# A top-k by bitwise search and matmuls in place of a top-k by maxima, and the next expert's transposes issued ahead of the down products

## The chip, the cores and the metric

One core of one Trainium2 chip. The metric is the device time of one launch in microseconds (us). All arithmetic is in float32. The engines are TensorE (PE; its weight loads are listed as PEld), VectorE (DVE), ScalarE (ACT), GpSimd (POOL) and SyncE (SP), which issues most of the DMAs. Each engine runs its own instruction stream; they meet at semaphores (`then_inc`, `wait_ge`).

## The reference

One layer of a diffusion backbone over 2048 tokens of width 1024: modulated RMSNorm, three token mixers (gated DeltaNet, Hyena, short convolution), a gated residual, and then the part that the change is about, an expert-choice mixture of experts (16 experts, 256 tokens each), followed by a final RMSNorm.

```python
def expert_choice_moe(h, router_w, w_gate, w_up, w_down):
    cap = CAPACITY_FACTOR * n // N_EXPERTS                      # 2 * 2048 // 16 = 256
    aff = jax.nn.softmax((h @ router_w).astype(jnp.float32), axis=-1)
    top_val, top_idx = lax.top_k(jnp.swapaxes(aff, 1, 2), cap)  # each expert takes its 256 best tokens
    xe = h[bidx, top_idx]
    hid = jax.nn.silu(jnp.einsum('becd,edf->becf', xe, w_gate)) * jnp.einsum('becd,edf->becf', xe, w_up)
    ye = jnp.einsum('becf,efd->becd', hid, w_down) * top_val[..., None].astype(h.dtype)
    return jnp.zeros_like(h).at[bidx, top_idx].add(ye.astype(h.dtype))
```

The order of an expert's 256 tokens doesn't matter to the output, since each row is added back to its own token.

## The kernel before

The kernel is a sequence of blocks; each ends with a barrier of all engines. Three of them matter here.

The **mixer's output stage** (L1720 to L1907) goes over 16 tiles of 128 tokens. TensorE makes `merged @ w_out` in two halves (`out_half`), VectorE and GpSimd form the new residual `x1` and the normalised row `h2`, TensorE transposes `h2` (`turn`, L1782) and makes the 16 router logits (`route`, L1792), VectorE and ScalarE the softmax in `ex` (L1841 to L1847). `turn_aff` transposes the 128x16 result (L1799), and VectorE copies it into `affT`, 16 experts by 2048 tokens (L1858). SyncE stores `x1` and `h2` in DRAM (`x1_d`, `h2_d`).

The **expert block** (from L1910) starts with the top-k. VectorE goes 32 times round `max` (the 8 largest of each of the 16 rows, L1951), `max_index` (where they are, L1954) and `match_replace` (they become -1, L1957). ScalarE copies each 8 values and 8 indices (L1986, L1987) to `vals` and `idxf`. TensorE transposes the lists with four small products (L2005, L2006), and VectorE copies them to `idxP` and `valP`, two columns of 128 tokens per expert (L1959, L1960).

Then sixteen experts, two per turn of a loop. GpSimd gathers an expert's 256 rows of `h2_d` with two indirect DMAs (L2050), one expert ahead. TensorE transposes them (16 transposes into banks 0 to 3, L2017), ScalarE copies them to the single buffer `xeT` (L1995), TensorE makes gate and up for six slices `f` of the hidden width, 32 instructions each, in banks 4 and 5 (L2025); ScalarE makes the sigmoid (L1999), VectorE two products (L1967, L1969) to `hid`. TensorE makes four down products of 6 x 2 instructions in banks 6 and 7 (L2036), VectorE scales them with the router value `valP` and the gate into `ye` (L1975), and GpSimd adds the rows to `x1_d` with two indirect DMAs (L2061). SyncE loads the weights: gate and up (3 MB each) are double buffered in `wgu`, down (3 MB) is single in `wd`; `wgu_free` and `wd_free` are raised by TensorE when it is done with a buffer (L1933, L1935). A float32 product is two weight loads and two passes on TensorE, a transpose one.

The **last block** reads `x1_d` back, normalises and stores.

The order on TensorE within an expert is the order of the code:

```python
pe.wait_ge(xe_in[b], i * 32 + 32)      # rows gathered
...                                    # 16 transposes
pe.wait_ge(xe_cp, at * 4 + 8)          # ScalarE's four copies
pe.wait_ge(wgu_in[b], i * 32 + 32)
...                                    # gate and up
pe.wait_ge(wd_in, at * 16 + 16)
pe.wait_ge(hid_ok, at * FT + FT + 2)   # VectorE's last hid
...                                    # down
```

## Time and profile before

| | us |
|---|---|
| median of 3 runs (lowest to highest) | 5180.27 (5178.26 to 5183.38) |
| the profiled execution, its own time | 5179.65 |
| its span in the profile | 5178.1 |
| TensorE busy | 4342.4 (84%) |
| VectorE busy | 1385.6 (27%) |
| ScalarE busy | 815.8 (16%) |
| GpSimd busy | 733.5 (14%) |
| DMA | 468 MB, 90 GB/s on average |

In the rows, a group reads: line, engine, operation, written tile <- read tiles, shapes, count | busy us, mean ns of one | idle time of the engine before them and what ended it. A line of the timeline is start, length, engine, line, operation, with the idle time before it in brackets. "x48" in a timeline is that many instructions run together. The granted clock is a share of full speed: 1.00 is 2.4 GHz, 0.50 is 1.2 GHz.

### The profile page before, as it was taken

To read this page: it belongs to the slowest core of one execution; us is meant where nothing else is said; L and a number is where in the kernel's file an instruction comes from. 1 tells how busy PE (TensorE), PEld (TensorE's weight loads), DVE (VectorE), ACT (ScalarE), POOL (GpSimd) and SP (SyncE) were. 2 spreads that over 40 slices of the span, in tenths; PEclk is the share of its full clock that TensorE was granted. 3 is DMA by queue.
4 is the path that set the end of the run, shared out by engine and by line. 5 is a ranking of instruction groups with operands and counts; after the bars stand their busy time and mean duration, and the time that the engine had idled before them with its cause. 6 is when DMAs were issued, how large, how long until landed. Compare 5 with 4: busy or idle time off the path is not lost. (4 is left out here: it accounts for less than half of the span.)

```text
span 5178.1 us, 49192 instructions
## 1 busy us (share of the span) xinstructions
PE 4342.4 (84%) x17543; PEld 2720.7 (53%) x17543; DVE 1385.6 (27%) x2250; ACT 815.8 (16%) x1538; POOL 733.5 (14%) x663
## 2 busy tenths in 40 slices
PE   7588888799999999877299999989900999999993
PEld 5344443599999844333144444435500777666662
DVE  1422222354555412232300000002289111111112
ACT  0244334122222111001100000001100000000002
POOL 0022233122222200001200000002200000000000
PEclk9799999899999999989599999999955999999997
DMA  6321111111111100254410000023330355554444
GB/s 239 135 61 49 48 53 46 63 53 57 61 53 61 53 25 14 67 157 124 148 33 27 24 26 26 24 68 134 113 130 1 105 178 178 178 178 169 161 151 142
DMA packets 253186, 468.13 MB, mean 90 GB/s; under 512 B 18964, under 2 KB 124092, under 8 KB 252992
## 3 DMA queue, kind: packets, MB, share of 16 engines
q1 hardware_dynamic: 218399, 366.54, 20.9%
q0 software_dynamic: 20560, 70.83, 5.0%
q10 hardware_dynamic: 14160, 29.89, 1.7%
q8 instruction: 40, 0.66, 0.1%
q14 instruction: 27, 0.21, 0.0%
HBM read 356.57 MB, written 110.62 MB: 90 GB/s over the span
## 5 line engine op out<-in xcount | busy, mean ns | idle before, releaser
L1666 PE MATMUL bank<-hT,gw 128*128 128x512 f32 x1536 | 678.6, 595 | 14.6 <-DMA bw<-in_w_branch_c 11.2
L2025 PE MATMUL bank<-xeT,wgu 128*128 128x256 f32 x3072 | 669.1, 380 | 14.6 <-ACT xeT L1995 14.6
L2025 PEld LDWEIGHTS bank<-xeT,wgu 128*128 128x128 f32 x3072 | 583.7, 190 | 97.5 <-issue 18.5
L500 PE MATMUL bank<-hT,wq 128*128 128x512 f32 (+1 forms) x1216 | 512.7, 577 | 9.6 <-DMA wq<-in_w_in 7.3
L1666 PEld LDWEIGHTS bank<-hT,gw 128*128 128x128 f32 x1536 | 292.2, 191 | 386.2 <-issue 386.2
L500 PEld LDWEIGHTS bank<-hT,wq 128*128 128x128 f32 x1216 | 237.1, 198 | 255.2 <-issue 249.2
L2036 PE MATMUL bank<-wd,hid_e 128*128 128x512 f32 x768 | 333.9, 594 | 22.1 <-DVE hid_e L1969 22.1
L1168 PE MATMUL bank<-hT,wh 128*128 128x512 f32 x768 | 336.4, 597 | 12.5 <-DMA wh<-in_w_in 9.4
L1697 DVE TENSOR_TENSOR pr<-sg_m,bank 128x512 f32<-128x512 f32 x96 | 66.0, 687 | 833.2 <-ACT sg_m L1682 833.2
L2036 PEld LDWEIGHTS bank<-wd,hid_e 128*128 128x128 f32 x768 | 144.6, 190 | 204.6 <-issue 176.0
L1168 PEld LDWEIGHTS bank<-hT,wh 128*128 128x128 f32 x768 | 145.6, 191 | 196.9 <-issue 196.9
L1773 PE MATMUL bank<-wo,mt 128*128 128x512 f32 x512 | 227.4, 598 | 16.4 <-DMA wo<-in_w_out 16.4
L884 PE MATMUL bank<-Eb,TT 128*128 128x128 f32 x1728 | 218.2, 279 | 20.3 <-DVE Eb L1086 20.3
L884 PE MATMUL bank<-Tb,N 128*128 128x128 f32 x1728 | 228.0, 277 | 0.3 <-ACT Tb L974 0.3
L884 PEld LDWEIGHTS bank<-Eb,TT 128*128 128x128 f32 x1728 | 206.8, 191 | 23.9 <-DVE Eb L1086 23.4
L1967 DVE TENSOR_TENSOR gm<-sgm,bank 128x256 f32<-128x256 f32 x96 | 40.4, 421 | 658.3 <-ACT sgm L1999 658.3
L884 PEld LDWEIGHTS bank<-Tb,N 128*128 128x128 f32 x1728 | 209.5, 192 | 3.6 <-ACT Tb L974 3.6
L2005 PE MATMUL bank<-eye,idxf 16*128 16x16 f32 x2 | 0.5, 273 | 239.6 <-ACT idxf L1987 239.6
L978 ACT ACTIVATE TT<-bank 128x512 f32<-128x512 f32 x216 | 129.0, 597 | 392.0 <-PE bank L890 389.5
L1682 ACT ACTIVATE sg_m<-bank 128x512 f32<-128x512 f32 x96 | 57.3, 597 | 780.0 <-PE bank L1669 779.9
L600 POOL TENSOR_SCALAR sg<-tmp 128x512 f32<-128x512 f32 (+1 forms) x76 | 104.6, 1376 | 508.3 <-DVE tmp L663 429.4
L2061 POOL DMA_INDIRECT x_d<-ye,idc x32 | 51.2, 1599 | 843.4 <-DVE ye L1975 843.4
(279 smaller groups left out, 4846.5 us busy)
## 6 DMA issues: line engine op xcount, KB each, us to landing
wgu<-in_exp_w_gate SPq DMA_DIRECT2D x16, 3072.0 KB, 23.1
wgu<-in_exp_w_up SPq DMA_DIRECT2D x16, 3072.0 KB, 30.4
wd<-in_exp_w_down SPq DMA_DIRECT2D x16, 3072.0 KB, 13.4
ada<-in_ada_w SPq DMA_DIRECT2D x12, 2048.0 KB, 8.9
gw<-in_w_in SPq DMA_DIRECT2D x27, 512.0 KB, 5.6
fa_d<-az ACTq DMA_DIRECT2D x48, 264.0 KB
sp_in<-fa_d SPq DMA_DIRECT2D x66, 192.0 KB, 4.1
kT<-kT_d SPq DMA_DIRECT2D x36, 256.0 KB, 2.8
```

Source lines behind the costliest of these rows:

```text
L500: last = pe.matmul(PS[u % 4][:, 0:width(n)], wq[:, kind, k, :], hT[:, k, toff(n):toff(n) + width(n)], start=(k == 0), stop=(k == KD - 1))
L600: pool.tensor_scalar_max(sg[:, u % 4, 0:w], tmp[:, u % 4, 0:w], CLAMP).then_inc(clamp_ok, 1)
L884: last = pe.matmul(b4(bank)[:, h, :], lhsT[:, h, :], rhs[:, h, :] if len(rhs.shape) == 3 else rhs, start=True, stop=True)
L978: act.activation(flat(TT, e), PS[2 * (e % 2) + 1][:, :], ACT.Copy).then_inc(TT_ok, 1)
L1168: last = pe.matmul(PS[u % 4][:, :], wh[:, kind, k, :], hT[:, k, toff(n + 1):toff(n + 1) + TW], start=(k == 0), stop=(k == KD - 1))
L1666: pe.matmul(g[:, :], gw[:, b, j, k, :], hT[:, k, toff(n + 1):toff(n + 1) + TW], start=(k == 0), stop=(k == KD - 1))
L1682: act.activation(sg[:, u % 2, :], PS[u % 4 * 2][:, :], ACT.Sigmoid).then_inc(sg_ok, 1)
L1697: dve.tensor_tensor(pr[:, u % 4, :], sg[:, u % 2, :], PS[u % 4 * 2 + 1][:, :], ALU.mult).then_inc(pr_ok, 1)
L1773: last = pe.matmul(PS[2 * (t % 2) + c][:, :], mt[:, t // 2 % 2, k, t % 2 * P:(t % 2 + 1) * P], wo[:, k, c * 512:(c + 1) * 512], start=(k = ...
L2025: last = pe.matmul(PS[4 + f % 2][:, g * CAP:(g + 1) * CAP], wgu[:, b, g, k, f * P:(f + 1) * P], xeT[:, k, :], start=(k == 0), stop=(k == K ...
L2036: last = pe.matmul(PS[6 + c][:, :], hid[:, f, j * P:(j + 1) * P], wd[:, f, c * 512:(c + 1) * 512], start=(f == 0), stop=(f == FT - 1))
L2061: pool.indirect_dma_start(x1_d, bass.IndirectOffsetOnAxis(idc[:, b, j:j + 1], 0), ye[:, j, :], None, compute_op=ALU.add).then_inc(ye_st, 16)
```

## The change

It has three parts.

1. In the mixer's output stage the softmax is kept by tile in `aff` (128 x 16 tiles x 16 experts); `turn_aff`, `ex` and `affT` are gone. A table `rt` (128 x 1104) is loaded. Rows of `h2_d` are 1040 long: the expert block stores a token's 16 router values behind its 1024 elements, so that a gather brings them along and `valP` is gone.
2. The top-k: `threshold` finds each expert's 256th largest value bit by bit. The values are laid out 128 wide, so that partition p holds expert p % 16. In each of 30 rounds VectorE compares 256 values per partition with a candidate and counts, TensorE adds the counts over the partitions of one expert with a block matrix, and VectorE keeps the bit or not. `slots` gives each chosen token its place in the list by products with triangular and counting matrices. `one_hot` and `listed`, each for eight experts, turn places into lists of token numbers: place = 16 * high + low, and a product of two one-hot matrices puts the token number at (high, low).
3. The experts: `turn`, the transposes of the next expert, is issued after gate/up and ahead of the down products. `xeT` has two buffers. The last two experts stand outside the loop.

```diff
# mixer's output stage
-                        pe.transpose(PS[7][0:NE, 0:P], ex[:, t % 2, :], eye[:, :]).then_inc(aff_tr, 1)
-                            dve.tensor_copy(affT[:, (t - 2) * P:(t - 1) * P], PS[7][0:NE, 0:P]).then_inc(affT_ok, 1)
+                    sp.dma_start(rt[:, :], A["t_rt"]).then_inc(rt_in, 16)
-                        sp.dma_start(h2_d[t * P:(t + 1) * P, :], h2[:, t % HB, :]).then_inc(h2_st[t % HB], 16)
+                        sp.dma_start(h2_d[t * P:(t + 1) * P, 0:D], h2[:, t % HB, :]).then_inc(h2_st[t % HB], 16)
# expert block, SyncE, ahead of the weight loads
+                    sp.dma_start(h2_d[:, D:D + NE].rearrange("(t p) e -> p t e", p=P), aff[:, :, :]).then_inc(aff_st, 16)
# VectorE: threshold
+                        for i in range(BITS):                     # BITS = 30
+                            bit = 1 << (BITS - 1 - i)
+                            c, nxt = cand[:, i % 3, :], cand[:, (i + 1) % 3, :]
+                            if i >= 1:
+                                dve.wait_ge(cand_ok, i)
+                            dve.tensor_scalar(hits[:, 0:2, :], affS[:, :, :], c.bitcast(F32), 0.0, ALU.is_ge, ALU.add, accum_out=votes[:, :]).then_inc(voted, 1)
+                            dve.tensor_scalar(nxt, c, bit | bit >> 1, None, ALU.bitwise_xor).then_inc(pair_ok, 1)
+                            dve.tensor_scalar(up[:, :], c, bit >> 1, None, ALU.bitwise_or).then_inc(pair_ok, 1)
+                            dve.wait_ge(vote_mm, i + 1)
+                            dve.tensor_scalar(full[:, :], PS[1][:, 0:1], CAP - 0.5, None, ALU.is_ge).then_inc(full_ok, 1)
+                            dve.wait_ge(full_ok, i + 1)
+                            dve.wait_ge(pair_ok, 2 * i + 2)
+                            dve.copy_predicated(nxt, full[:, :], up[:, :]).then_inc(cand_ok, 1)
# VectorE: slots (thrB, four counts, cntB, two masks, then eleven chained instructions of 128x256 or 128x512)
+                        for g, op in enumerate((ALU.is_gt, ALU.is_equal)):
+                            for h in range(2):
+                                dve.tensor_scalar(hits[:, 2 * g + h, :], affS[:, h, :], thr, 0.0, op, ALU.add, accum_out=cnt[:, 2 * g + h:2 * g + h + 1]).then_inc(cnt_ok, 1)
...
+                        link(dve.tensor_tensor(least[:, :, :], ties, wanted, ALU.min))
...
+                        link(dve.tensor_copy(digf[:, :], digu[:, :]))
# VectorE: one_hot(g), listed(g)
+                        for a in range(16):
+                            dve.scalar_tensor_tensor(hotA[:, :, :, a], high, float(a), index, ALU.is_equal, ALU.mult).then_inc(hot_ok, 1)
+                        for b in range(16):
+                            dve.tensor_scalar(hotB[:, :, :, b], low, float(b), None, ALU.is_equal).then_inc(hot_ok, 1)
...
+                        dve.tensor_tensor(own[:, :, :], PS[5][:, 0:P].rearrange("p (e b) -> p e b", b=16), own_e, ALU.mult).then_inc(z_ch, 1)
...
+                        dve.tensor_copy(idxP[:, :, g * 8:(g + 1) * 8], PS[6][:, 0:16].rearrange("p (j e) -> p j e", j=2)).then_inc(slots_ok, 1)
...
+                    threshold(); slots(); one_hot(0); listed(0); one_hot(1); listed(1)
+                    dve.sem_inc(hid_ok, 2)
# VectorE, experts
-                                dve.scalar_tensor_tensor(ye[:, j, c * 512:(c + 1) * 512], PS[6 + c][:, :], valP[:, j, ds(at, 1)], g2,
+                                dve.scalar_tensor_tensor(ye[:, j, c * 512:(c + 1) * 512], PS[6 + c][:, :], xe[:, b, j, ds(at + D, 1)], g2,
# TensorE
+                        for i in range(BITS):
+                            pe.wait_ge(voted, i + 1)
+                            pe.matmul(PS[1][:, 0:1], rt[:, T_BLK:T_BLK + P], votes[:, :], start=True, stop=True).then_inc(vote_mm, 1)
...
+                        for g in range(2):                        # slots
+                            for h in range(2):
+                                pe.matmul(PS[3 + g][:, 0:17 * NE], cntB[:, 2 * g + h, :], rt[:, (T_E0, T_E1)[h]:(T_E0, T_E1)[h] + 17 * NE], start=(h == 0), stop=False)
+                        for g in range(2):
+                            pe.wait_ge(mask_ok, g + 1)
+                            pe.matmul(PS[3 + g][:, 0:TILES * NE], rt[:, T_SU:T_SU + P], mask[:, g].rearrange("p t e -> p (t e)"), start=False, stop=True).then_inc(pos_mm, 1)
+                    def lists(g):
+                        pe.wait_ge(hot_ok, 32 * g + 32)
+                        for t in range(TILES):
+                            last = pe.matmul(PS[5][:, 0:P], hotA[:, t].rearrange("p e a -> p (e a)"), hotB[:, t].rearrange("p e b -> p (e b)"),
+                                             start=(t == 0), stop=(t == TILES - 1))
+                        last.then_inc(list_mm, 1)
+                        pe.wait_ge(spread_ok, g + 1)
+                        pe.matmul(PS[6][:, 0:16], spread[:, :, :].rearrange("p r b -> p (r b)"), rt[:, T_PLACE:T_PLACE + 16], start=True, stop=True).then_inc(idx_mm, 1)
...
+                    def expert(i, b, more):
+                        at = i * 2 + b
+                        pe.wait_ge(xe_cp, at * 4 + 4)
+                        pe.wait_ge(wgu_in[b], i * 32 + 32)
...                                                               # gate and up as before
+                        if more:
+                            turn(i + b, 1 - b, at + 1)
+                        pe.wait_ge(gu_mm, at * FT + FT)
+                        pe.sem_inc(wgu_free, 1)
+                        pe.wait_ge(wd_in, at * 16 + 16)
+                        pe.wait_ge(hid_ok, at * FT + FT + 2)
...                                                               # down as before
+                    threshold(); slots(); lists(0); turn(0, 0, 0); lists(1)
+                    with pe.Fori(0, NE // 2 - 1) as i:
+                        for b in range(2):
+                            expert(i, b, True)
+                    expert(NE // 2 - 1, 0, True)
+                    expert(NE // 2 - 1, 1, False)
# GpSimd, ahead of the first gather
                     pool.wait_ge(slots_ok, 1)
+                    pool.wait_ge(aff_st, 16)
```

ScalarE follows the same order: the six sigmoids of an expert, then the four copies of the next expert's transposes.

## Rows read from the trace of the kernel before

**Rows 1.** The page: 40 slices, busy tenths and granted TensorE clock.
```profile
PE   7588888799999999877299999989900999999993
...
PEclk9799999899999999989599999999955999999997
```

**Rows 2.** Windows: stretch, us, busy by engine, clock, DMA share, GB/s.
```profile
3700.00:3750.00 50.00, 50.00 (x173) 26.45 (x172) 10.73 (x24) 9.28 (x24) 14.09 (x6) 1.00 0.23 84
3800.00:3810.00 10.00, 0.00 (x0) 0.00 (x0) 9.32 (x8) 0.31 (x2) 0.00 (x0) 0.50 0.98 382
3810.00:3850.00 40.00, 0.00 (x0) 0.00 (x0) 37.20 (x28) 1.84 (x12) 0.00 (x0) 0.50 0.00 0
```

**Rows 3.** Timeline (start, us, instruction) around the top-k stage's two ends.
```profile
3767.24 0.23 DVE L1847 TENSOR_SCALAR ex<-ex,sm 128x16 f32<-128x16 f32 x1
...
3767.53 0.38 PE L1799 MATMUL bank<-eye,ex 128*16 128x128 f32 x1 [1.32 <-DVE ex L1847]
3767.95 0.28 DVE L1858 COPY affT<-bank 16x128 f32<-16x128 f32 x1 [0.47 <-PE bank L1799]
3768.82 0.40 SPq L1933 DMA_DIRECT2D wgu<-in_exp_w_gate  x1
...
4009.41 0.17 DVE L1959 CAST idxP<-bank 128x32 uint32<-128x32 f32 x1
4009.51 0.17 DVE L1960 COPY valP<-bank 128x32 f32<-128x32 f32 x1
...
4017.79 3.67 PE L2017 MATMUL bank<-eye,xe 128*128 128x128 f32 x16 [9.64 <-DMA xe<-h_d,idc]
...
4022.23 1.22 PE L2025 MATMUL bank<-xeT,wgu 128*128 128x256 f32 x2 [0.77 <-ACT xeT L1995]
```

**Rows 4.** Groups of the top-k stage: count, busy us, mean ns, idle before.
```profile
L1951 DVE MAX8 m<-affT 16x8 f32<-16x2048 f32 x32 | 73.0, 2282 | 8.7 <-DVE affT L1957 7.5 <-DVEq L1939 1.3
...
L1957 DVE MATCH_REPLACE8 affT<-m,affT 16x2048 f32<-16x2048 f32 x32 | 72.5, 2264 | 0.0
...
L1954 DVE MATCH_VALUE_LOAD i<-m,affT 16x8 f32 x32 | 2.5, 79 | 4.7
```

**Rows 5.** Timeline of TensorE's products over three experts.
```profile
4067.23 20.87 PE L2036 MATMUL bank<-wd,hid_e 128*128 128x512 f32 x48 [1.39 <-DVE hid_e L1969]
4088.40 1.97 PE L2017 MATMUL bank<-eye,xe 128*128 128x128 f32 x16 [0.30 <-PE bank L2036]
4091.29 41.70 PE L2025 MATMUL bank<-xeT,wgu 128*128 128x256 f32 x192 [0.92 <-ACT xeT L1995]
4134.38 20.87 PE L2036 MATMUL bank<-wd,hid_e 128*128 128x512 f32 x48 [1.38 <-DVE hid_e L1969]
4156.07 1.96 PE L2017 MATMUL bank<-eye,xe 128*128 128x128 f32 x16 [0.83 <-PE bank L2036]
```

**Rows 6.** The page: DMA issues, KB each, median us to landing.
```profile
wd<-in_exp_w_down SPq DMA_DIRECT2D x16, 3072.0 KB, 13.4
```

**Rows 7.** Groups of VectorE by shape.
```profile
L1967 DVE TENSOR_TENSOR gm<-sgm,bank 128x256 f32<-128x256 f32 x96 | 40.4, 421 | 658.3 <-ACT sgm L1999 658.3
...
L418 DVE TENSOR_SCALAR xb<-xb,ss 128x1024 f32<-128x1024 f32 x18 | 12.4, 749 | 15.6 <-ACT ss L397 15.6
...
L277 DVE TENSOR_SCALAR turns<-arg 64x512 f32<-64x512 f32 x8 | 3.4, 419 | 0.3
...
L762 DVE TENSOR_TENSOR gx<-gl,dtb 128x160 f32<-128x160 f32 x1 | 0.3, 325 | 0.0
...
L759 DVE TENSOR_SCALAR beta<-gl 128x160 f32<-128x160 f32 x1 | 0.2, 244 | 0.0
```

**Rows 8.** Timeline at the mixer stage's tail, TensorE at half clock.
```profile
3762.61 3.49 PEld L1792 LDWEIGHTS bank<-rw,h2T 128*128 128x128 f32 x16 [1.58 <-ACT h2T L1878]
...
3766.81 0.19 ACT L1871 ACTIVATION_READ_ACCUMULATOR ex<-bank,mx 128x1 f32 x1
```

**Rows 9.** Timeline of GpSimd: the second gather of expert 2.
```profile
4102.98 0.95 POOL L2050 DMA_INDIRECT xe<-h_d,idc  x1 [0.30 <-issue]
```

More of the change, by code:

```diff
@@ L1719, in build @@
         fst = top.enter_context(ExitStack())
-        affT = sbt(fst, "affT", [NE, SEQ])
+        aff = sbt(fst, "aff", [P, TILES, NE])
+        rt = sbt(fst, "rt", [P, N_RT])
+        rt_in = sem("rt_in")
         fgb = sbt(fst, "fgb", [P, D])
@@ L1815, in _ @@
                             out_half(t, 1)
-                        if t >= 2:
-                            turn_aff(t - 2)
                         if 1 <= t <= TILES:
@@ L1924, in build @@
             dn_mm, ye_ok, ye_st, ye_free = sem("dn_mm"), sem("ye_ok"), sem("ye_st"), sem("ye_free")
+            hits = gm1[:, :, :].rearrange("p a (b t) -> p (a b) t", t=P)
+            cntB = sgm[:, :, :].rearrange("p a (b t) -> p (a b) t", t=P)
+            mask = hid[:, 0:2, :].rearrange("p g (t e) -> p g t e", e=NE)
+            least, slot, chosen = [hid[:, r, :].rearrange("p (t e) -> p t e", e=NE) for r in (2, 3, 4)]
+            own, spread = [hid[:, 5, h * P:(h + 1) * P].rearrange("p (e b) -> p e b", b=16) for h in range(2)]
+            hotA = ye[:, :, :].rearrange("p j (t e a) -> p (j t) e a", e=8, a=16)
+            hotB = xeT[:, 1, :, :].rearrange("p k (t e b) -> p (k t) e b", e=8, b=16)
             with nc.Block() as block:
@@ L1962, in _ @@
+                    threshold()
+                    slots()
+                    one_hot(0)
+                    listed(0)
+                    one_hot(1)
+                    listed(1)
+                    dve.sem_inc(hid_ok, 2)
                     with dve.Fori(0, NE // 2) as i:
@@ L2001, in _ @@
+                    with act.Fori(0, NE // 2 - 1) as i:
+                        for b in range(2):
+                            expert(i, b, True)
+                    expert(NE // 2 - 1, 0, True)
+                    expert(NE // 2 - 1, 1, False)
                 @block.tensor
                 def _(pe):
[L2003 to L2006 removed]
@@ new lines, in threshold @@
+                    def threshold():
+                        for h in range(2):
+                            last = pe.transpose(PS[0][:, h * P:(h + 1) * P], aff[:, h * 8:(h + 1) * 8, :].rearrange("p t e -> p (t e)"), eye[:, :])
+                        last.then_inc(affS_tr, 1)
+                        pe.wait_ge(rt_in, 16)
+                        for i in range(BITS):
+                            pe.wait_ge(voted, i + 1)
+                            pe.matmul(PS[1][:, 0:1], rt[:, T_BLK:T_BLK + P], votes[:, :], start=True, stop=True).then_inc(vote_mm, 1)
@@ new lines, in turn, with expert @@
+                    def turn(i, b, at):
+                        pe.wait_ge(xe_in[b], i * 32 + 32)
+                        for k2 in range(KD // 2):
+                            for k in (2 * k2, 2 * k2 + 1):
+                                for j in range(2):
+                                    last = pe.transpose(PS[k2][:, (k % 2 * 2 + j) * P:(k % 2 * 2 + j + 1) * P], xe[:, b, j, k * P:(k + 1) * P], eye[:, :])
+                            last.then_inc(xe_tr, 1)
+                    def expert(i, b, more):
+                        at = i * 2 + b
+                        pe.wait_ge(xe_cp, at * 4 + 4)
+                        pe.wait_ge(wgu_in[b], i * 32 + 32)
+                        for f in range(FT):
+                            pe.wait_ge(hid_ok, at * FT + f + 1)
+                            for g in range(2):
+                                for k in range(KD):
+                                    last = pe.matmul(PS[4 + f % 2][:, g * CAP:(g + 1) * CAP], wgu[:, b, g, k, f * P:(f + 1) * P], xeT[:, b, k, :],
+                                                     start=(k == 0), stop=(k == KD - 1))
+                            last.then_inc(gu_mm, 1)
+                        if more:
+                            turn(i + b, 1 - b, at + 1)
[3 more added lines that the diff above has]
+                        pe.wait_ge(hid_ok, at * FT + FT + 2)
+                        for m in range(4):
+                            j, c = m // 2, m % 2
+                            if m >= 2:
+                                pe.wait_ge(ye_ok, at * 4 + m - 1)
+                            for f in range(FT):
+                                last = pe.matmul(PS[6 + c][:, :], hid[:, f, j * P:(j + 1) * P], wd[:, f, c * 512:(c + 1) * 512],
+                                                 start=(f == 0), stop=(f == FT - 1))
+                            last.then_inc(dn_mm, 1)
+                        pe.wait_ge(dn_mm, at * 4 + 4)
+                        pe.sem_inc(wd_free, 1)
@@ L2042, in _ @@
+                    threshold()
+                    slots()
+                    lists(0)
+                    turn(0, 0, 0)
+                    lists(1)
+                    with pe.Fori(0, NE // 2 - 1) as i:
+                        for b in range(2):
+                            expert(i, b, True)
+                    expert(NE // 2 - 1, 0, True)
+                    expert(NE // 2 - 1, 1, False)
                 @block.gpsimd
```

182 lines of the change are left out of this document (91 added, 91 removed).

## The prediction

> **What bounds the kernel now.** I read the page's 40 slices first: TensorE is busy nearly everywhere, except around the 30th slice, where its row shows 0 and 0 and its granted clock is 0.5 [rows 1]. The windows say what that stretch is: VectorE busy 37.2 of 40 us, TensorE and DMA 0 [rows 2]. The timeline of its two ends gives its length. The mixer stage's last instruction ends at 3767.95 + 0.28 = 3768.23; the first gate/up product of expert 0 starts at 4022.23 [rows 3]. So 254.0 us pass in which TensorE does four tiny transposes and one expert's 16. The groups say what fills them: VectorE instructions of 2.26 to 2.28 us, 32 times each, in a chain (L1951 and L1957; L1954's find is as long) [rows 4]. Behind it come sixteen experts on TensorE. There the PE timeline repeats every 67.15 us (down product to down product), 0.5 more where the loop turns back: 1.96 transposes, 0.92 idle behind ScalarE's last copy, 41.70 gate and up, 1.39 idle behind VectorE's last hid, 20.87 down, and 0.3 or (loop back) 0.8 idle [rows 5]. Nothing else is late there: the first 15.7 MB of weights took from 3768.8 to about 3810 [rows 2, 3], and wd lands a median 13.4 us after issue, with 46 us before its product [rows 5, 6]. TensorE's own order is therefore the path in the experts, VectorE's in the top-k.
>
> **Part 1, removed: the top-k by maxima.** The whole 254.0 us goes, and the new chain is built up below from the same start (3768.23).
>
> Entry into the block until the first instruction: 0.6, as SyncE's (3768.82). Two transposes and one 256-wide copy from PSUM: at half clock two weight loads are 0.22 apart (16 in 3.49), the product ends some 0.11 behind the last, and a copy of that size is 0.42 by the 256-wide rows: 1.0 with hand-offs.
>
> The search is 30 rounds of a closed loop between VectorE and TensorE. One round: (a) the compare of 128x256 with a [128,1] pointer and an accumulator. No row has this form. L277 (512 wide) took 0.419 and L759 (160 wide) 0.244, 0.5 ns a column; the two-input L762 (160) and L1967 (256) 0.325 and 0.421, 1 ns a column. L418 (1024 wide, with a pointer) took 0.749, 0.24 over its columns at 0.5 ns. So 256 columns are 0.37 at the fast rate and 0.50 at the slow one [rows 7]. (b) the accumulator read: between 0.08, the tiny VectorE instruction of rows 4, and 0.19, ScalarE's own accumulator read [rows 8]. (c) TensorE: hand-off 0.05, a product as two load-and-product pairs 0.55, hand-off 0.04 [rows 3, 8]. The two tiny candidate updates (0.17 each) run beside it. (d) the test of the count and the predicated copy, 0.17 each as the tiny L1959 [rows 3], and 0.04 to 0.08 for each wait. Sum: 0.37 to 0.50, 0.08 to 0.19, 0.64, 0.42 to 0.50: 1.5 to 1.8, and I take 1.6, for a one-input compare should go at the fast rate. Thirty: 48. Bounds: 1.25 if the product is prompt (0.35) and the read is free, 2.1 if each of the three waits on VectorE costs the 0.23 that L1951 shows behind its two waits (7.5 us in 32) [rows 4]: 37 to 63 us.
>
> Slots: threshold spread 0.15; four counts of 128 columns at about 0.42 = 1.7; spread 0.46; then TensorE. A 512-column pass goes every 0.43 us at full clock (48 in 20.87), so 272 columns at half clock are 0.46, eight of them 3.65, and four passes of 256 columns 1.72, with hand-offs 5.5. Behind it eleven chained VectorE instructions, mostly 256 wide at 0.42 and 0.04 apart [rows 7]: 4.3. Together 12.1 (10 to 15).
>
> One-hots of experts 0 to 7: sixteen two-input instructions of 128 columns and sixteen one-input. By L762 (160 wide, 0.325) and L759 (0.244) they are 0.29 and 0.23 long. They have no wait between them, and such rows overlap: L1959 and L1960 are 0.17 long and start 0.10 apart [rows 3, 7]. So 0.22 and 0.16, 6.1 us; I take 7 for strided writes. Against this the Trainium skill, VectorE: DVE Perf Modes, The DRAIN you can't avoid, says that the next instruction doesn't start before the pipe is empty; by that the sum would be 8.3. The pair of rows disagrees with it, by 0.07 us per instruction, so I keep 7.
>
> Lists of experts 0 to 7: 16 products of 128 columns, two pairs each at 0.22: 7.1 at half clock. Their reduction: three VectorE instructions of about 0.33, a product 0.6, a copy 0.17: 1.8 with its waits. Now GpSimd may gather; from the copy's end to expert 0's transposes took 4017.79 - 4009.68 = 8.1, and the transposes 3.7 [rows 3]. Experts 8 to 15 have their one-hots made meanwhile (7 or 8.3, hidden in 11.8), but their products stand behind expert 0's transposes in TensorE's queue, and hid_ok is raised only after them: 7.1 + 1.8 more before the first gate/up product. ScalarE's copies of expert 0 lie beside that.
>
> Sum: 0.6 + 1.0 + 48 + 12.1 + 7 + 7.1 + 1.8 + 8.1 + 3.7 + 7.1 + 1.8 = 98.3. The gain is 254.0 - 98.3 = **155.7**. Ends: 82 (votes 37, lists of the second half at full clock, fewer gaps) and 120.
>
> Two covers to check. The weights: expert 0's gate/up and down and expert 1's gate/up needed 41 us; the aff store (2,048 pieces of 64 B) goes ahead of them on SyncE's queue. Even if it costs 10 us they are in by 3820, against a first use at 3866. With the cover gone, had the new chain only the same 41 us, the store's whole 10 us would show. The table load (565 KB) lies behind wo's in the stage before.
>
> **Part 2, the mixer stage.** turn_aff and the affT copy go. TensorE is busy 50 of 50 us there [rows 2] and a transpose takes it about 0.11 us (16 in 1.97) [rows 5]: 14 x 0.11 = 1.5; one more at its tail, 0.1; and at the very end 3768.23 falls back to 3767.47, 0.76 [rows 3]. Together **2.4**. The h2 store, its rows now 4,160 B apart, is the same 4 KB per row.
>
> **Part 3, transposes ahead of the down products.** At the 15 boundaries TensorE now runs gate/up, the next 16 transposes, down, gate/up. Gone: the 0.92 behind ScalarE, because the copies lie under 20.87 us of down products, and the 1.39 behind VectorE, because the transposes fill it. They take 16 x 0.11 = 1.75 in a busy stream rather than 1.97, and start without the pipe draining. So down starts 1.6 to 1.75 instead of 1.39 after gate/up, and 1.96 + 0.92 disappear behind it: 2.5 to 2.65 each. Taking **2.5**: 15 x 2.5 = **37.5** (32 to 41). The 0.3 and 0.8 idle at the end of down stay; they come from waiting for its own product and the loop. Are the gathered rows there in time? The second was asked for at 4102.98, 15 us after the previous down ended [rows 5, 9], and takes about 6; the transposes now come 42 us after it. POOL's queue (scatter, wait for it, gather) is as before. SyncE's queue is unchanged in order; wgu_free comes 1.7 us later but SyncE stands at wd_free then. wd now has 43 us rather than 46 for its load. Reading the value from the gathered row costs the 0.75 us instruction nothing (a pointer either way), and 64 B more per row is 1.6%. The unrolled last pair replaces one loop turn.
>
> **Sum.** 155.7 + 2.4 + 37.5 = 195.6. The profiled execution took 5179.65 us (span 5178.1), 0.6 below the median 5180.27; the median's forecast is 5180.3 - 195.6 = 4984.7, say **4985**.
>
> **Rivals.**
> - *The hand-offs are dearer* (2.3 us and more per round: several semaphore waits in a row, an accumulator read that blocks). For it: 0.23 us behind two waits on VectorE [rows 4]; against it TensorE's 0.06 behind L1847 and VectorE's 0.04 behind TensorE [rows 3]. The Trainium skill, VectorE: DVE Perf Modes, Two Vector instructions with no wait between them, counts an accumulator output as two instructions; ScalarE's rows show the pair, and my (b) holds it. Time: 30 x 0.7 to 1.5 more, 5006 to 5030. Chance 0.14.
> - *The reorder gives nothing* in the experts: the transposes hold back down by what they save, or gate/up's loads wait. Against it, 0.92 and 1.39 are real idle time of TensorE [rows 5]. Time 4985 + 37 = 5022. Chance 0.05.
> - *The search is cheaper*: TensorE at full clock in the rounds, prompt products, 1.2 us each, lists at full clock: 98 falls to 80, 4966 and below. For it, the rounds give TensorE something to do; against it, no row shows the clock in such a loop, and the top-k stands at 0.50 [rows 1, 2]. Chance 0.09.
> - *Slower than before*: the gather comes late in the experts. Now transposes in front of down wait for it, and down with them. Down ended, the rows are in after some 21 us, against 42: it must come 21 us later before it costs anything, and 13 us at each of 15 boundaries more to eat 195. So above 5190 only from 34 us late on. Nothing on POOL's queue is new there. Chance 0.01.
> - *The maxima aren't the path*, the weights are: excluded by [rows 2], DMA is 0 from 3810 on. It would leave the top-k as it is, 5140; chance below 0.01.
>
> **How the numbers follow.** My forecast's chance is 0.70; its own range is 4968 to 5003 (votes 1.35 to 1.9, slots and lists +-4, boundaries +-4). The cheap and the dear search take the range to 4962 and 5010, which leaves out about 2 in 10. All cases but the fourth, and something unforeseen, are faster by over 0.2% (10 us, about what a measurement tells from no change): faster 0.97, same 0.01, slower 0.02.
>
> **What would show it.** From the stage's last softmax instruction to the first gate/up product some 98 us; rounds 1.6 us apart, with TensorE's part 0.6; a list product group of 7 us before and one after expert 0's transposes; gate/up starting 0.3 or 0.8 us after down; no idle before down; down-to-down 64.7 and 65.1. Wrong: rounds over 2 us, one-hots over 0.35 us each (two to four times 7 us), the second lists' one-hots later than the transposes, or a wait for xe in front of down.

## The result, and the profile after

| | before | after |
|---|---|---|
| median, us | 5181.83 (4 runs, 5178.26 to 5186.61) | 4975.4 (4 runs, 4970.01 to 4981.11) |
| ratio (95% interval) | | 0.9601 (0.9585 to 0.9618) |
| the profiled execution, its span | 5179.65, 5178.1 | 4970.01, 4968.5 |
| VectorE busy | 1385.6 | 1209.0 |
| TensorE busy | 4342.4 | 4362.6 |

The kernel became 206.4 us faster. The forecast of 4985 (4962 to 5010) is 9.6 us too high, and its sum of 195.6 us of gain is 14 us short of the 209.6 by which the profiled span shrank. The page after, 40 slices, busy tenths of TensorE and its granted clock:

```profile
PE   7588898699999999977639999999995999999993
...
PEclk9799999899999999999959999999996999999996
```

The two slices at 0, with clock 0.5, around the 30th in [rows 1] are now one slice of 5 tenths busy at 0.6. From here the traces are put beside each other by stage:

| stretch, us | before | after | gain | forecast |
|---|---|---|---|---|
| start to the mixer's output stage (unchanged code) | 3490.3 | 3487.6 | 2.7 | 0 |
| output stage, to its last instruction | 277.9 | 275.3 | 2.6 | 2.4 |
| top-k, to the first gate/up product | 254.0 | 91.6 | 162.4 | 155.7 |
| sixteen experts, to the last down product's end | 1076.4 | 1034.4 | 42.0 | 37.5 |
| tail | 79.5 | 79.6 | -0.1 | 0 |

The first line is the difference of two executions, not of two kernels: the output stage starts between 3487.6 and 3504.1 in the profiles of this study. The top-k stage repeats within 0.6 us and the experts within 0.1 wherever their code is the same, so the experiments are read by them.

The top-k stage in the timeline of the kernel after (start, length, engine, line): its start, one round of the search, the slots, the lists.

```profile
3762.67 0.23 DVE L1851 TENSOR_SCALAR aff<-aff,sm 128x16 f32<-128x16 f32 x1
...
3766.06 0.48 DVE L1974 TENSOR_SCALAR_CACHE_REDUCE gm<-affS,cand 128x256 f32<-128x256 f32 x1
3766.46 0.08 DVE L1974 DVE_READ_ACCUMULATOR gm<-affS,cand 128x1 f32 x1
...
3766.60 0.59 PE L2093 MATMUL bank<-votes,rt 128*128 128x1 f32 x2 [1.03 <-DVE gm L1974]
3767.23 0.16 DVE L1978 TENSOR_SCALAR full<-bank 128x1 uint32<-128x1 f32 x1 [0.55 <-PE bank L2093]
3767.42 0.22 DVE L1981 COPY_PREDICATED_SCALAR cand<-full,up 128x1 uint32 x1
3767.67 0.48 DVE L1974 TENSOR_SCALAR_CACHE_REDUCE gm<-affS,cand 128x256 f32<-128x256 f32 x1
...
3823.59 3.60 DVE L2019 SCALAR_TENSOR_TENSOR ye<-digf,rt 128x128 f32<-128x128 f32 x16
3827.03 2.29 DVE L2021 TENSOR_SCALAR xeT<-digf 128x128 f32<-128x128 f32 x16
3829.37 6.38 PEld L2109 LDWEIGHTS bank<-xeT,ye 128*128 128x128 f32 x32 [10.49 <-DVE xeT L2021]
3829.37 6.57 PE L2109 MATMUL bank<-xeT,ye 128*128 128x128 f32 x32 [10.09 <-DVE xeT L2021]
...
3837.49 0.17 DVE L2035 CAST idxP<-bank 128x16 uint32<-128x16 f32 x1 [0.49 <-PE bank L2113]
...
3845.99 3.30 PE L2120 MATMUL bank<-eye,xe 128*128 128x128 f32 x16 [8.54 <-DMA xe<-h_d,idc]
...
3849.14 3.74 PE L2109 MATMUL bank<-xeT,ye 128*128 128x128 f32 x32
...
3854.41 0.17 DVE L2035 CAST idxP<-bank 128x16 uint32<-128x16 f32 x1 [0.49 <-PE bank L2113]
...
3854.50 0.70 PE L2131 MATMUL bank<-xeT,wgu 128*128 128x256 f32 x2
```

The stage begins where L1851 ends, 3762.90, and ends at 3854.50. The round starts at 3766.06 and the next at 3767.67: 1.61 us. In it the compare and its accumulator read take 0.48, and 0.06 later TensorE's product begins, whose two pairs take 0.59. The test follows 0.04 later (0.16), then the copy (0.22 from 3767.42), and 0.03 behind it the next compare.

The experts, TensorE's timeline of the kernel after:

```profile
3854.50 41.71 PE L2131 MATMUL bank<-xeT,wgu 128*128 128x256 f32 x192
3896.05 1.91 PE L2120 MATMUL bank<-eye,xe 128*128 128x128 f32 x16
3897.79 20.77 PE L2145 MATMUL bank<-wd,hid_e 128*128 128x512 f32 x48
3919.10 41.70 PE L2131 MATMUL bank<-xeT,wgu 128*128 128x256 f32 x192 [0.54 <-PE bank L2145]
3960.64 1.91 PE L2120 MATMUL bank<-eye,xe 128*128 128x128 f32 x16
3962.38 20.77 PE L2145 MATMUL bank<-wd,hid_e 128*128 128x512 f32 x48
3984.02 41.70 PE L2131 MATMUL bank<-xeT,wgu 128*128 128x256 f32 x192 [0.87 <-PE bank L2145]
```

Against [rows 5]: no idle time in front of the transposes, none between them and the down products, none behind ScalarE's copies. What is left is 0.54, or 0.87 where the loop turns back, and its releaser is TensorE's own product. Down starts are 64.59 and 64.92 apart, where they were 67.15 and 67.6. The waits from 3854 to 4870 (total, times, longest) say how rare anything else is:

```profile
PE bank L2131 <- PE bank L2145: 9.7, 15, 0.9
...
PE bank L2145 <- DVE hid_e L2052: 1.5, 1, 1.5
```

The one wait for VectorE is the last expert's, which has no transposes behind its gate/up.

### The profile page after: what moved, and what is told of

The parts are those of the page before. It is cut to its first block and busy times, and to the rows that moved or that the text cites. A ratio compares the mean times of both kernels' runs of the same rounds, so it can differ in the third digit from the quotient of the medians.

```text
span 4968.5 us, 49038 instructions
## 1 busy us (share of the span) xinstructions
PE 4362.6 (88%) x17666; PEld 2748.0 (55%) x17666; DVE 1209.0 (24%) x2348; ACT 794.2 (16%) x1465; POOL 736.0 (15%) x664
## 3 DMA queue, kind: packets, MB, share of 16 engines
q1 hardware_dynamic: 220607, 367.24, 21.8%
## 5 line engine op out<-in xcount | busy, mean ns | idle before, releaser
L2073 ACT ACTIVATE sgm<-bank 128x256 f32<-128x256 f32 x96 | 36.8, 383 | 939.4 <-PE bank L2131 939.4
## 6 DMA issues: line engine op xcount, KB each, us to landing
wd<-in_exp_w_down SPq DMA_DIRECT2D x16, 3072.0 KB, 13.4
```

## The experiments

Three kinds of doubt were left. Does the ledger by stage say which part of the change brought what? Are the terms inside the search what the timeline suggests? And what is the 0.54 and 0.87 that TensorE still waits in each expert? The column "before" is the median of the kernel before, timed beside the run; the last column has the ratio with its interval.

| run | median, us (lowest to highest) | before | ratio (95%) |
|---|---|---|---|
| turn behind down | 5012.69 (5005.45 to 5018.34) | 5181.02 | 0.9663 (0.9644 to 0.9681) |
| before, turn ahead of down | 5137.86 (5136.35 to 5149.19) | 5181.02 | 0.9908 (0.9891 to 0.9925) |
| 15 rounds | 4953.58 (4947.62 to 4956.54) | 5181.02 | 0.9555 (0.9539 to 0.9572) |
| buffers freed elsewhere | 4959.34 (4957.77 to 4968.42) | 5181.02 | 0.9570 (0.9552 to 0.9589) |
| votes in bfloat16 | 4964.31 (4960.09 to 4965.28) | 5179.17 | 0.9581 (0.9565 to 0.9597) |
| lists first | 4976.91 (4973.88 to 4977.32) | 5179.17 | 0.9606 (0.9590 to 0.9622) |
| gather after slice 3 | 4976.94 (one run) | 5179.17 | |
| gather after slice 5 | 4993.67 (one run) | 5179.17 | |
| three together | 4946.00 (4942.36 to 4959.93) | 5178.36 | 0.9550 (0.9537 to 0.9563) |
| after, again | 4977.18 (4964.27 to 4980.96) | 5178.36 | 0.9600 (0.9586 to 0.9615) |

### The reorder undone

```diff
-                        if more:
-                            turn(i + b, 1 - b, at + 1)
                         pe.wait_ge(gu_mm, at * FT + FT)
...
                         pe.wait_ge(dn_mm, at * 4 + 4)
                         pe.sem_inc(wd_free, 1)
+                        if more:
+                            turn(i + b, 1 - b, at + 1)
```

> The changed kernel with one edit: the next expert's 16 transposes stand behind the down products again; top-k and mixer stage stay new. Theory (two idle times of TensorE per boundary went, 0.92 and 1.39 us, and the pipe's fill between the groups): each of the 15 boundaries is longer by 2.5 to 2.7 us, so 38 to 40 us slower than the changed kernel, about 5014 us, ratio to before 0.968. Rival (the experts gained because TensorE ran clocked up or the weights came earlier, not by the order): less than 10 us slower.

Measured 5012.69, 37.3 us above the kernel after; the experts take 1070.2 instead of 1034.4, 35.8 more, which is a little under the 38 to 40 expected. TensorE's timeline of this kernel has the old waits again:

```profile
4044.91 20.87 PE L2143 MATMUL bank<-wd,hid_e 128*128 128x512 f32 x48 [1.38 <-DVE hid_e L2052]
4065.93 1.94 PE L2120 MATMUL bank<-eye,xe 128*128 128x128 f32 x16
4068.79 41.70 PE L2131 MATMUL bank<-xeT,wgu 128*128 128x256 f32 x192 [0.92 <-ACT xeT L2066]
4111.87 20.87 PE L2143 MATMUL bank<-wd,hid_e 128*128 128x512 f32 x48 [1.38 <-DVE hid_e L2052]
4133.05 1.96 PE L2120 MATMUL bank<-eye,xe 128*128 128x128 f32 x16 [0.31 <-PE bank L2143]
4136.02 41.70 PE L2131 MATMUL bank<-xeT,wgu 128*128 128x256 f32 x192 [1.02 <-ACT xeT L2066]
```

So the place of the transposes is worth 35.8 us in the experts, as two waits that it removes. The rival "the reorder gives nothing" is out. Of the whole 42.0 it leaves 6.2, which were in the kernel before and are not in this one. About 1.9 is expert 0's gate/up, 41.7 long here; in the trace of the kernel before it took 43.61, because the clock rose only some 4 us after its start (0.50 from 4022.2 to 4026.0, 0.97 from 4026 to 4028). The next run shows that it can be 41.7 behind the old top-k too. The rest is 0.3 per boundary (periods 66.96 and 67.24 against 67.15 and 67.6). Most of it lies at the loop's turn: the branch now falls between transposes and gate/up, where TensorE waits for ScalarE in any case (1.02 instead of 0.92), and the 0.83 of [rows 5] is 0.31. The other boundary is shorter too, by 0.19: the transposes begin 0.15 instead of 0.30 behind down. The kernel before has a wait for ScalarE's copies ahead of each four transposes that this one hasn't; whether that is the 0.15 was not tested.

### The reorder alone, in the kernel before

The transposes of the kernel before, issued ahead of the down products, with the single `xeT` and the old top-k:

```diff
-                    with pe.Fori(0, NE // 2) as i:
...
+                    turn(0, 0, 0)
+                    with pe.Fori(0, NE // 2 - 1) as i:
+                        for b in range(2):
+                            expert(i, b, True)          # gate/up, turn of the next, down
+                    expert(NE // 2 - 1, 0, True)
+                    expert(NE // 2 - 1, 1, False)
# ScalarE: the six sigmoids, then the next expert's four copies into the one xeT
```

> The kernel before with one edit: the next expert's transposes are issued ahead of the down products (xeT stays single). Theory (the two parts are independent): 15 boundaries x 2.5 to 2.7 = 38 to 40 us faster than before, about 5142 us, ratio 0.992 to 0.993; together with the first run the parts add up to the whole. Rival (the reorder needs the new top-k, or the second xeT buffer): less than 20 us faster.

Measured 5137.86: 43.2 below the kernel before, a little more than the 38 to 40 expected; by the traces the experts take 1034.4 instead of 1076.4, 42.0 less. The periods are 64.57 and 64.92, the same as in the kernel after to 0.03 us. The second `xeT` buffer therefore brings nothing: ScalarE's copies lie behind the last gate/up product either way.

Expert 0's gate/up, in the kernel before and in this one:

```profile
4022.23 43.61 PE L2025 MATMUL bank<-xeT,wgu 128*128 128x256 f32 x192 [0.77 <-ACT xeT L1995]
```
```profile
4033.18 41.70 PE L2034 MATMUL bank<-xeT,wgu 128*128 128x256 f32 x192 [0.87 <-ACT xeT L1992]
```

Both stand behind the old top-k. Here the clock rose during the transposes (1.00 from 4032 to 4034), in the kernel before some 4 us into gate/up. So 1.7 of the 42.0 (1.9 of gate/up, less the 0.2 by which down starts later behind it) hang on when the clock rises. With the old top-k it had risen in time in one of two profiles, with the new one in all ten; whether the change makes it sure is not shown.

With the run above, what one part gives doesn't depend on the other: the experts have the whole 42.0 with the old top-k, and the top-k stage takes 92.0 with the old order. The medians agree once the 6.2 that both runs hold is counted once: 168.3 (from the kernel before to the run above) + 43.2 - 6.2 = 205.3, against 206.4.

### Half of the rounds

Fifteen rounds instead of thirty. This leaves out the threshold's 15 low bits, so that the lists are partly of other tokens.

```diff
-            BITS = 30
+            BITS = 15
-                            bit = 1 << (BITS - 1 - i)
+                            bit = 1 << (29 - i)
+                            low = bit >> 1 if i < BITS - 1 else 0
```

> The changed kernel with 15 rounds of the search instead of 30; the 15 low bits of each threshold are left out, so lists hold 256 of a few more tokens. Theory (the rounds are a closed loop on the path, 1.61 us each, and nothing beside them is late): 15 x 1.614 = 24.2 us faster than the changed kernel, about 4951 us, and the top-k stage 91.6 - 24.2 = 67.4 us long. Rival (the weight loads, which took 42 us from the same start, or the aff store become the bound): less than 20 us faster, with a wait for wgu or for the aff store in the chain.

Measured 4953.58, 21.8 below the kernel after; by the traces the stage is 67.5 instead of 91.6, 24.1 less, which is 15 rounds of 1.61. So the search lies on the path with its whole length and nothing else becomes late when it is shorter, the first weights neither. Each round left out was worth its 1.61 us.

### The buffers freed by the engines that wait for the products anyway

TensorE raises `wgu_free` and `wd_free` after a wait for its own last product. Here ScalarE raises the one and VectorE the other, each behind the wait that it has already.

```diff
# TensorE
-                        pe.wait_ge(gu_mm, at * FT + FT)
-                        pe.sem_inc(wgu_free, 1)
...
-                        pe.wait_ge(dn_mm, at * 4 + 4)
-                        pe.sem_inc(wd_free, 1)
# ScalarE, in the sigmoids' loop
                             act.wait_ge(gu_mm, at * FT + f + 1)
+                            if f == FT - 1:
+                                act.sem_inc(wgu_free, 1)
# VectorE, in the loop over the down products
                                 dve.wait_ge(dn_mm, at * 4 + m + 1)
+                                if m == 3:
+                                    dve.sem_inc(wd_free, 1)
```

> The changed kernel, but wgu_free is raised by ScalarE and wd_free by VectorE, each behind a wait for TensorE's products that it makes anyway; TensorE no longer waits for its own products. Theory (the 0.54 and 0.87 us that TensorE is idle between down and gate/up are mostly the wait for its own last product): idle falls to about 0 and 0.4, 15 x 0.4 to 0.5 = 6 to 8 us faster than the changed kernel. Rival (this idle time is the loop's branch and the issue of the next group's waits): no difference, within 2 us.

Measured 4959.34, 16 below the kernel after. TensorE's timeline of this kernel:

```profile
3897.57 1.91 PE L2124 MATMUL bank<-eye,xe 128*128 128x128 f32 x16
3899.32 20.77 PE L2147 MATMUL bank<-wd,hid_e 128*128 128x512 f32 x48
3919.92 41.60 PE L2135 MATMUL bank<-xeT,wgu 128*128 128x256 f32 x192
3961.36 1.91 PE L2124 MATMUL bank<-eye,xe 128*128 128x128 f32 x16
```

Gate/up begins before the modelled end of the last down product (3920.09), and every period is 63.79, the loop's turn included. The experts take 1021.0: 13.4 less. That is about twice what I expected. I had counted on the wait of some 0.5 us and not on the loop's 0.35, which I took for the branch's own cost. It isn't one that shows without the wait: the period with the loop's turn is 63.79 like the others. All the idle time behind down was 9.7 us in the kernel after (the waits above). Some 2.5 more come from gate/up starting 0.17 ahead of down's modelled end at each of 15 boundaries, and 1.4 from the gate/up products, 41.44 instead of 41.54 from their start to that of the transposes. Two waits went at once, the one behind gate/up and the one behind down; by these places nearly all of the gain is the second's, but they were not taken out one by one.

### The votes in bfloat16

The counts, up to 256, and the 0/1 block matrix are exact in bfloat16. The float32 product is two weight loads and two passes, this one is one.

```diff
-            affS, votes = sbt(st, "affS", [P, 2, P]), sbt(st, "votes", [P, 1])
+            affS, votes = sbt(st, "affS", [P, 2, P]), sbt(st, "votes", [P, 1], mybir.dt.bfloat16)
+            blk, blk_ok = sbt(st, "blk", [P, P], mybir.dt.bfloat16), sem("blk_ok")
...
-                            pe.matmul(PS[1][:, 0:1], rt[:, T_BLK:T_BLK + P], votes[:, :], start=True, stop=True).then_inc(vote_mm, 1)
+                            pe.matmul(PS[1][:, 0:1], blk[:, :], votes[:, :], start=True, stop=True).then_inc(vote_mm, 1)
```

> The changed kernel, but the votes and the block matrix are bfloat16 (counts up to 256 and 0/1 are exact in it), so that a round's product is one load-and-product pair instead of two. Theory (TensorE's 0.59 us of a round are two pairs 0.22 to 0.27 apart and a latency of about 0.3): a round falls from 1.61 to 1.30 to 1.40 us, 30 rounds by 6 to 9 us, about 4968 us. Rival (the 0.59 us are hand-off and fill, the second pair is hidden): a round stays above 1.55 us and the gain under 2 us.

Measured 4964.31, about 11 below the kernel after; the stage takes 80.0 instead of 91.6, 11.6 less. A round in the timeline of this kernel:

```profile
3774.14 0.09 DVE L1978 DVE_READ_ACCUMULATOR gm<-affS,cand 128x1 bf16 x1
...
3774.28 0.19 PE L2098 MATMUL bank<-votes,blk 128*128 128x1 bf16 x1 [1.03 <-DVE gm L1978]
3774.51 0.16 DVE L1982 TENSOR_SCALAR full<-bank 128x1 uint32<-128x1 f32 x1 [0.16 <-PE bank L2098]
3774.70 0.22 DVE L1985 COPY_PREDICATED_SCALAR cand<-full,up 128x1 uint32 x1
3774.95 0.48 DVE L1978 TENSOR_SCALAR_CACHE_REDUCE gm<-affS,cand 128x256 f32<-128x256 f32 x1
```

Only the product's length changed, 0.59 to 0.19, and the round with it: 1.61 to 1.21. The hand-offs are 0.06 and 0.04 as before. That is more than the 1.30 to 1.40 us per round and the 6 to 9 us that I expected: one pair less took away 0.40, where I had counted 0.22 to 0.27 for it. The pair that is left is in bfloat16 as well, so the run can't tell how much the number of pairs gave and how much the type. Of the 1.61, TensorE's product was 0.59, the compare 0.54 to TensorE's start, and the chain of test and copy 0.48 with its waits. This also bears on the prediction's step (c), which had 0.55 for the product as two load-and-product pairs: the size was right and there are two pairs, but what one of them costs in such a loop stays open.

### The second lists ahead of expert 0's transposes

```diff
                         last.then_inc(list_mm, 1)
+                        if g == 1:
+                            turn(0, 0, 0)
                         pe.wait_ge(spread_ok, g + 1)
...
-                    turn(0, 0, 0)
                     lists(1)
```

> The changed kernel, but TensorE makes the list products of experts 8 to 15 ahead of expert 0's transposes, and their last small product behind them. Theory (the products can run while the gather is on its way, and only the transposes and the copies of expert 0 lie behind it): the stage from the last softmax instruction to the first gate/up product falls from 91.6 by 1 to 3 us, which only the trace can show. Rival (the second lists' one-hots are ready too late, so that the transposes now wait for the products): the stage stays the same or grows by up to 3 us.

Measured 4976.91, which the medians don't tell from the kernel after. The trace does: the stage takes 89.75, where it took 91.4 to 92.0 in six profiles with the other order. TensorE in this kernel's timeline:

```profile
3853.02 6.38 PE L2109 MATMUL bank<-xeT,ye 128*128 128x128 f32 x32 [5.99 <-DVE xeT L2021]
3859.24 1.91 PE L2122 MATMUL bank<-eye,xe 128*128 128x128 f32 x16
...
3860.99 0.29 PE L2115 MATMUL bank<-rt,hid_e 128*128 128x16 f32 x2
...
3862.18 1.99 PE L2133 MATMUL bank<-xeT,wgu 128*128 128x256 f32 x8 [0.90 <-ACT xeT L2066]
```

The list products fill the time in which GpSimd's gather is under way, but they now run at half clock (6.38 instead of 3.74), and the transposes behind them at full clock (1.91 instead of 3.30). By the 8.33 us that the gather took in the kernel after, the rows of expert 0 were there some 3.7 us before its transposes; the order and the clock together leave 1.85.

### How late the gather may come

GpSimd asks for the next expert's rows after the third, or after the fifth, of the six gate/up slices:

```diff
+                            pool.wait_ge(gu_mm, at * FT + 5)      # 3 in the other run
                             gather(ds((at + 1) % NE, 1), 1 - b, at + 2)
```

> The changed kernel, but GpSimd issues the next expert's gather only when three of six gate/up slices are made, 20.8 us after gate/up's start. Theory (the rows land 8 to 9 us after the gather's start and are first needed at 41.6): no difference in the experts' stage, periods stay 64.6 and 64.9 us. Rival (the slack is smaller than that, since scatter and gather share a queue): over 5 us slower.

> The same with the gather behind five slices, 34.7 us after gate/up's start. Theory: the rows land at 43 to 44 us, 1.5 to 2.5 us behind the transposes' place, and since the transposes stand ahead of down this goes straight into the period: 15 x 1.5 to 2.5 = 22 to 38 us slower, with TensorE waiting for the DMA of xe. Rival (ahead of down there is still cover): under 5 us slower.

After slice 3 (20.8 us ahead of the end of gate/up) nothing changes: 4976.94, the experts 1034.4. After slice 5 it is 4993.67 and 1051.5, 1.14 us per boundary. TensorE and GpSimd in that kernel's timeline:

```profile
3962.09 0.18 POOL L2166 COPY idc<-idxP 128x2 uint32 x1 [32.36 <-PE bank L2131]
...
3969.70 1.97 PE L2120 MATMUL bank<-eye,xe 128*128 128x128 f32 x16 [0.92 <-DMA xe<-h_d,idc]
3971.50 20.77 PE L2145 MATMUL bank<-wd,hid_e 128*128 128x512 f32 x48
3993.14 41.70 PE L2131 MATMUL bank<-xeT,wgu 128*128 128x256 f32 x192 [0.87 <-PE bank L2145]
```

The rows are in 7.6 us after the copy of the indices. In the kernel after, that copy begins at 3931.57 and the transposes at 3960.64, 29.1 later: 21.5 us of slack, where the forecast had 21. Each of the two was run once; their traces' stages are compared with the kernel after's. The wait stands in front of the transposes as the rival "slower than before" had it. I had sized this run too high (the wait is 0.9, since a slice of gate/up, 6.95 us, covers nearly the whole gather).

### Three together

The freed buffers, the bfloat16 votes and the lists first, in one kernel, and the kernel after beside it:

> The changed kernel with three edits together: wgu_free and wd_free raised by ScalarE and VectorE (period 63.79 us in its own run), votes in bfloat16 (round 1.22 us), the second lists' products ahead of expert 0's transposes. Theory (the three lie in different stretches of one path and add up): experts 1034.4 to 1021.0, top-k stage 91.6 by 11.9 and 1.9 to 78, so 27 us faster than the changed kernel, about 4948 us. Rival (one of them uncovers a wait that was hidden behind another, such as the gather or the weights): under 20 us faster.

> The changed kernel itself, on the same chip and in the same rounds as the combined version, for the comparison of the two: 4970 to 4981 us as before, top-k stage 91.5 to 92.0 us, experts 1034.4 us.

Measured 4946.0 against 4977.18, 31.2 less. By the traces the stage takes 77.4 instead of 91.4 and the experts 1021.0 instead of 1034.4: 14.0 + 13.4 = 27.4, against 26.9 for the three by their own traces (11.6, 1.9 and 13.4): they add up. It beats the kernel before by 4.5%. The other 3.8 us lie in the spread of the medians.

## Why the prediction came out as it did

Its sign, its mechanism and its range held; the time was 9.6 us lower than forecast. Term by term, from the timeline above, forecast to measured:

| term | forecast | measured |
|---|---|---|
| entry | 0.6 | 0.29 |
| transposes and copy of aff | 1.0 | 1.19 |
| thirty rounds | 48 | 48.46 |
| slots | 12.1 | 10.75 |
| one-hots of experts 0 to 7 | 7 | 5.78 |
| their lists, and reduction | 7.1 + 1.8 | 6.61 + 1.68 |
| gather | 8.1 | 8.33 |
| expert 0's transposes | 3.7 | 3.15 |
| second lists, and reduction | 7.1 + 1.8 | 3.77 + 1.59 |
| sum | 98.3 | 91.6 |

- *The search* was right as a whole, with two errors that happened to cancel. The compare is 0.48 long, which is the slow rate that (a) kept as its upper end, not the 0.37 that I took to be likelier. The read that (b) added to it starts 0.40 after the compare's start and ends with it, so it adds nothing, where I had 0.08 to 0.19. The Trainium skill, VectorE: DVE Perf Modes, Two Vector instructions with no wait between them, counts the accumulator output as two instructions; the trace agrees, there are two, and they overlap. The rival "dearer hand-offs" falls: no wait in the round costs over 0.06, and the copy, which stands behind two waits (`full_ok`, `pair_ok`), starts 0.03 behind the test. So two waits alone don't cost the 0.23 that stood in front of L1951; what did stays open.
- *The rival "cheaper search"* had two halves. The round stayed at half clock throughout and was 1.61, so its first half is wrong. Its second, lists at full clock, held for the second lists alone.
- *The second lists* are the largest miss, 3.3 of the 6.7 us in the stage. The sum priced them at half clock, and they ran at full. The windows of the kernel after (stretch, us, busy by engine, clock, DMA share, GB/s):

```profile
3803.00:3813.00 10.00, 3.53 (x12) 3.02 (x12) 6.21 (x39) 0.00 (x0) 0.00 (x0) 0.50 0.21 82
3818.00:3820.00 2.00, 1.28 (x6) 0.79 (x4) 0.75 (x3) 0.00 (x0) 0.00 (x0) 0.98 0.00 0
3833.00:3835.00 2.00, 2.00 (x11) 2.00 (x11) 0.00 (x0) 0.00 (x0) 0.00 (x0) 0.50 0.00 0
3835.00:3837.00 2.00, 0.94 (x8) 0.75 (x6) 0.95 (x3) 0.00 (x0) 0.00 (x0) 0.97 0.00 0
3845.00:3847.00 2.00, 1.00 (x5) 1.01 (x6) 0.00 (x0) 0.00 (x0) 1.07 (x2) 0.50 0.55 131
3850.00:3852.00 2.00, 2.00 (x20) 2.00 (x19) 0.00 (x0) 1.24 (x1) 0.00 (x0) 1.00 0.02 8
```

  In the search TensorE is busy 3.5 of 10 us at 0.50, the 1.2 GHz level. It rises to 0.98 in the slots, is back at 0.50 all through the first lists, stands at 0.97 when these are done and little runs, and at 0.50 again for the first transposes. It rose during the transposes, so the second lists got 1.00. When it rises differs by execution: the two list groups took 6.57 and 3.74 here, and 5.34 and 4.68 in the run with the gather after slice 3, whose top-k is the same code. The stage's sum hardly does (91.4 to 92.0 in six profiles with the same top-k). So the size was off, and a forecast to the microsecond wasn't to be had from [rows 1, 2]; half way between the two rates would have been the better choice.
- *Slots*, 1.35 less: the four mask passes took 1.03 rather than 1.72, at the risen clock, and the four counts stand 0.27 apart where the sum had 0.42 each.
- *One-hots*: they start 0.215 (two inputs) and 0.13 apart (one input) though 0.37 and 0.27 long, so they overlap by more than the pair of rows in [rows 3]. Against the Trainium skill, VectorE: DVE Perf Modes, The DRAIN you can't avoid, by whose rule the prediction worked out 8.3, 5.78 was measured; the measurement decides, and the exception that the same section makes for a next instruction that isn't held is what these rows show. The lengths are above the 0.29 and 0.23 that the sum had for them from unstrided rows, by 0.08 and 0.04, which may be the strided writes; the spacing is what counts, and it is under the 0.22 and 0.16 of the sum. So the 0.9 that I added for strides is the larger part of the miss, and what the strides cost was not measured.
- *The mixer stage*: 2.6 for 2.4.
- *The experts*: 40.3 in the 15 periods, 2.68 each, and 1.7 around expert 0's gate/up, which ran at full clock throughout. The sum had nothing for the second, and it may be luck: with the old top-k one of two profiles has it too (the reorder alone). Of the boundary, the transposes and the wait for ScalarE took 2.89 with them, and down starts 43.28 instead of 43.09 after gate/up, 0.19 lost where I had 0.2 to 0.36; down to the next gate/up or transposes is 0.02 longer on average. I had worked out 2.5 to 2.65 and took the lower.
- *The idle time behind down* is still there, as forecast, and a little longer (0.54 and 0.87; 0.3 and 0.8 before). But the prediction took it as given, and it was 13.4 us that could be had.
- *Covers*: the DMA share is 0.19 from 3805 to 3806, 0.05 to 3807 and 0 behind it, so the value store and the 15.7 MB were in by 3807, up to 44 us after the stage's first DMA at 3763.18; before it took some 41 (from 3768.82; the share is 0.52 from 3809 to 3810 and 0 behind it). The store costs at most 3 us, against the 10 allowed for, and hides, with the first use at 3854.5. GpSimd's slack is measured above. The search's 30 rounds were never a question of the weights: even with 15 the first use waits for the list.
- *The rest*, 2.7 us of the span, is unchanged code and not the change. That much of the 14 us by which the gain passed the sum is chance, and the clock's 1.7 may be.

## What to carry to other kernels

When a stage is a chain on one engine while another idles, count the rounds of the replacement and price one round from its hand-offs (0.03 to 0.06 us here) and its shortest instructions; the largest of them is worth a cheaper type (a float32 product of one column is 0.59 us at half clock, a bfloat16 one 0.19). Put work whose input is ready between two dependent groups of the engine that sets the end; it removes the wait in front of the one and the copy behind the other, 2.4 to 2.7 us per expert here (the order undone, and the order alone), for 1.75 of work that had to be done anyway. And never let that engine wait for its own product only to raise a semaphore: an engine that waits for the same product already can raise it for nothing (13.4 us in 15 boundaries here).

## What the runs showed of the hardware that was not expected

- A VectorE compare with an accumulator goes by the two-input rate of about 1 ns a column, though it reads one tensor: 0.48 us for 256 columns, 0.34 for 128. The accumulator's read starts 0.40 after the compare and takes 0.08.
- VectorE instructions without a wait between them start closer than they are long: 0.07 apart for the tiny candidate updates (0.15 long), 0.13 and 0.215 for the one-hots (0.27 and 0.37 long).
- TensorE's wait for its own last product cost 0.54 us, and 0.87 at the end of a loop; without it both were 0.
- The granted clock lagged behind what the engine did: a stretch in which TensorE was busy 0.94 of 2 us had it full (0.97 at 3835 to 3837), and the one before it, busy throughout, had half (0.50 at 3833 to 3835).
- GpSimd's copy of 128x2 indices takes 0.18 us, but 2.10 at 3841.26, while VectorE ran its sixteen one-input one-hots (3841.04 to 3843.34). It ended with them. A copy started beside the two-input one-hots (3837.73) took 0.18. The Trainium skill, SBUF — State Buffer, SBUF: two separate sides, says that the two engines share a pair of ports under an exclusive lock, held for one whole instruction by a VectorE instruction in a two-port mode, or by one with two SBUF inputs against a GpSimd one that reads SBUF. The trace agrees on the first in part: the copy was held up, but until the last of the sixteen was done and not for one of them (0.27). On the second it disagrees: the two-input one-hots read two SBUF tensors, the first of them had begun 0.15 before the copy (3837.58), the copy reads one too, and it took its 0.18. That gather was expert 1's and hid; expert 0's, one step earlier, was not touched.
